# Sums over partitions of an adaptive-norm modulation: TensorE columns, or accumulating transfers in DRAM on GpSimd's queue

## What is computed

```python
c_act = jax.nn.silu(c)
mod = (c_act @ mod_w[layer] + mod_b[layer]).reshape(B, N_SUB, 3, D_MODEL)   # first block, 3 sublayers a layer
shift, scale, gate = mod_j[:, 0], mod_j[:, 1], mod_j[:, 2]
h = rmsnorm(x, g) * (1 + scale[:, None, :]) + shift[:, None, :]             # a sublayer's input
x = x + MACARON_W * g * swiglu(h, ...)                                      # g = 1 + gate
mod = c_act @ ada_w[i] + ada_b[i]                                           # second block, 2 sublayers a layer
```

## Time and profile before

| | |
|---|---|
| median of 3 runs | 2444.95 us |
| the profiled execution | 2440.32 us |
| its span, first to last instruction | 2438.7 us |
| TensorE busy, granted clock | 93% of the span, 0.947 |
| VectorE, ScalarE, GpSimd busy | 67%, 50%, 15% |
| DMA engines, mean | 219 GB/s, 65% of 16 engines' time |
| TensorE's share of the chain that ended last | 83% |

### The profile page before, as it was taken

The page is one execution under the profiler, slowest core; times in us unless marked ns, Lnnn a source line. Parts: engine busy times, 40 slices in busy tenths (PEclk is TensorE's granted clock), DMA queues, the critical chain, the costliest instruction groups (busy, mean ns, idle before and its releaser), DMA issues.

```text
span 2438.7 us, 37573 instructions
## 1 busy us (share of the span) xinstructions
PE 2262.4 (93%) x14486; PEld 2054.7 (84%) x14486; DVE 1635.7 (67%) x1943; ACT 1216.4 (50%) x1898; POOL 366.2 (15%) x513
## 2 busy tenths in 40 slices
PE   2999999999999995999988999998999799998998
PEld 2998977998999894898866998987987798876987
DVE  6677754767776755766875776775766776654654
ACT  2544455544553454544554554535545554565543
POOL 0111100111121003111000120800210221000210
PEclk9999999999999997999977999999999899988999
DMA  8789872878897951798664578512778378441653
GB/s 326 258 287 325 284 256 91 283 266 319 262 320 257 281 189 43 253 316 284 213 240 143 176 265 277 180 35 87 242 288 247 98 255 287 133 131 54 188 198 104
DMA packets 295522, 532.98 MB, mean 219 GB/s; under 512 B 10065, under 2 KB 185564, under 8 KB 295388
## 3 DMA queue, kind: packets, MB, share of 16 engines
q1 hardware_dynamic: 262396, 358.05, 44.8%
q0 software_dynamic: 32992, 173.09, 20.0%
HBM read 530.00 MB, written 1.11 MB: 218 GB/s over the span
## 4 chain that ended last, share of the span: by engine, by line
PE 83%; DVE 7%; ACT 5%; issue 3%; DMA 2%; SPq 0%; POOL 0%; DVEq 0%; ACTq 0%
PE bk L1340 12%; PE bk L1341 12%; PE bk L1342 12%; PE bk L1239 9%; PE bk L1241 9%; PE bk L1240 8%; PE bk L1391 4%; PE bk L1589 2%; PE bk L1284 1%; DVE w_lo L1706 1%; PE bk L1227 1%; PE bk L1229 1%; PE bk L1228 1%; DVE mod_acc L1725 1%; PE bk L1317 1%
## 5 line engine op out<-in xcount | busy, mean ns | idle before, releaser
L1706 DVE TENSOR_TENSOR w_lo<-raw,w_hi 128x1024 fp32r<-128x1024 f32 (+5 forms) x720 | 833.2, 1186 | 520.9 <-ACT w_hi L791 519.3
L791 ACT ACTIVATE w_hi<-raw 128x1024 fp32r<-128x1024 f32 (+5 forms) x720 | 683.0, 976 | 683.0 <-PE bk L1241 335.7
L1340 PE MATMUL bk<-a_hi,w_hi 128*128 128x256 f32 x2332 | 665.0, 285 | 5.2 <-DVE a_lo L1791 5.2
L1341 PE MATMUL bk<-a_lo,w_hi 128*128 128x256 f32 x2332 | 663.5, 285 | 0.0
L1342 PE MATMUL bk<-a_hi,w_lo 128*128 128x256 f32 x2332 | 663.2, 284 | 0.0
L1340 PEld LDWEIGHTS bk<-a_hi,w_hi 128*128 128x128 f32 x2332 | 451.6, 194 | 6.5 <-DVE a_lo L1791 4.0
L1341 PEld LDWEIGHTS bk<-a_lo,w_hi 128*128 128x128 f32 x2332 | 451.6, 194 | 0.0
L1342 PEld LDWEIGHTS bk<-a_hi,w_lo 128*128 128x128 f32 x2332 | 451.4, 194 | 0.0
L1725 DVE SCALAR_TENSOR_TENSOR mod_acc<-mod_raw,cact,mod_acc 128x1536 f32<-128x1536 f32 x182 | 329.9, 1813 | 35.4 <-DMA mod_raw<-in_ada_w 20.4
L1241 PE MATMUL bk<-w_hi,hid_lo 128*128 128x512 f32 x832 | 327.4, 394 | 0.0
L1239 PE MATMUL bk<-w_hi,hid_hi 128*128 128x512 f32 x832 | 324.3, 390 | 3.0 <-DVE w_lo L1706 3.0
(11 more groups left out here) (341 smaller groups left out, 3221.9 us busy)
## 6 DMA issues: line engine op xcount, KB each, us to landing
raw<-in_ffn_w SPq DMA_DIRECT2D x128, 1024.0 KB, 5.8
mod_raw<-in_ada_w POOLq DMA_DIRECT2D x128, 768.0 KB, 6.2
raw<-in_ffn_w_gu SPq DMA_DIRECT2D x88, 1024.0 KB, 7.6
mod_raw<-in_mod_w POOLq DMA_DIRECT2D x80, 768.0 KB, 6.9
raw<-in_ffn_w_down SPq DMA_DIRECT2D x40, 1024.0 KB, 7.1
first_mod<-in_mod_w SPq DMA_DIRECT2D x16, 768.0 KB, 10.0
raw<-in_sb_w_qkv SPq DMA_DIRECT2D x12, 1024.0 KB, 6.6
raw<-in_conv_w_pw SPq DMA_DIRECT2D x12, 1024.0 KB, 5.5
```

The source lines that it names most:

```text
L791: ins = act.activation(o(w_hi[:, p % OPS, :]), r(raw[:, c % RAWS, :]), ACT.Copy)
L1340: pe.matmul(o, wh, a_hi[:, f, :], start=(f == 0), stop=False)
L1341: pe.matmul(o, wh, a_lo[:, f, :], start=False, stop=False)
L1706: ins = dve.tensor_tensor(o(w_lo[:, p % OPS, :]), r(raw[:, c % RAWS, :]), o(w_hi[:, p % OPS, :].bitcast(F32)), ALU.subtract)
```

## The change

Groups 1 to 13 no longer go through the 24 products. When a group's 16 units are in, GpSimd stores mod_acc (1.5 MB) to a DRAM buffer folds, 128 rows of 3072. Seven transfers within DRAM then add the lower half of the remaining rows to the upper half, with an accumulating DMA on GpSimd's queue: 64 rows onto 64, then 32, 16, 8, 4, 2 and 1. A ninth transfer loads the single row that is left as a tile mod_row of 24 rows x 128, and TensorE transposes that tile into 24 PSUM columns. Each of the nine steps waits on the queue for the one before it. Group 0 keeps the 24 products.

```diff
+        mod_row = sb("mod_row", [MODC // P, P])
+        folds = nc.dram_tensor("folds", (2, P, MODC), F32).ap()
+        fold_done = sem("fold_done")
+        STEPS = 9
...
+            def fold(g, i):
+                if g is None:
+                    return
+                if i == 0:
+                    pool.wait_ge(mod_used, 2 + UNITS * (g + 1))
+                    if g > 1:
+                        pool.wait_ge(fold_done, 16 * STEPS * (g - 1))
+                    pool.dma_start(folds[g % 2], mod_acc[:, :]).then_inc(fold_done, 16)
+                    return
+                pool.wait_ge(fold_done, 16 * (STEPS * (g - 1) + i))
+                if i == STEPS - 1:
+                    pool.wait_ge(mod_ready, g)
+                    pool.dma_start(mod_row[:, :], folds[g % 2, 0].rearrange("(j p) -> j p", p=P)).then_inc(fold_done, 16)
+                    return
+                n = P >> i
+                wide = min(MODW, n * MODC // 16)
+                flat = folds[g % 2].rearrange("k f -> (k f)")
+                upper, lower = (flat[a * MODC:(a + n) * MODC].rearrange("(q f) -> q f", f=wide) for a in (0, n))
+                pool.dma_start(upper, lower, accum_op=ALU.add, max_dma_last_dim=4 * MODW).then_inc(fold_done, 16)
...
+            def mod_sum(g, w):
+                is_free(pe, w)
+                if g == 0:
...
+                else:
+                    pe.wait_ge(fold_done, 16 * STEPS * g)
+                    ins = pe.transpose(mod_out(w), mod_row[:, :], ident[0:MODC // P, 0:MODC // P])
+                ins.then_inc(turn_done, 1)
+                k.add("turn", 1)
```

The ffn1 stage on GpSimd's queue, and VectorE's new wait before it overwrites mod_acc:

```diff
-                    mod_rest(g, lambda i, b: hid_low(n + 2 * i + b, 2 * i + b, b))
+                    for j in range(KD):
+                        mod_next(g, j + 1)
+                        hid_low(n + j, j, j % 2)
+                        fold(st["late"], j + 1)
+                    fold(g, 0)
                     for b in range(3):
                         if b:
                             mod_next(g + 1, b)
                         hid_low(n + 8 + b, 8 + b, b % 2)
+                        fold(g, b + 1)
                     gate_tile(st["n"])
...
-                    for r in range(3, KD):
+                    for i in (4, 5, 6):
+                        fold(g, i)
+                    mod_next(g + 1, 3)
+                    for i in (7, 8):
+                        fold(g, i)
+                    for r in range(4, KD + 1):
                         mod_next(g + 1, r)
-                    mod_next(g + 1, KD)
+                    fold(g + 1, 0)
...
                 if isinstance(r, int) and r == 0:
+                    if g >= 2:
+                        dve.wait_ge(fold_done, 16 * (STEPS * (g - 2) + 1))
                     dve.tensor_scalar(a, src, cc[:, 0:1], None, ALU.mult).then_inc(mod_used, 1)
```

On TensorE the call moves from the start of a stage, and from job 8 of ffn1, into later jobs; keep_busy takes its place at the start:

```diff
-                if st["late"]:
-                    mod_sum(st["late"], w)
-                elif g:
+                if g:
+                    turned()
                     is_free(pe, w)
-                    keep_busy(job_banks(w)[:, 3, :], 16 if after(g) == "post" else 6)
+                    keep_busy(job_banks(w)[:, 3, :], 16 if after(g) == "post" else 8)
...
+                    if beside is not None and q == n // 2:
+                        mod_sum(beside, w - 1)
...
-                        gate_up(c + 2 * b, w + b, 0, second=(lambda: mod_sum(st["groups"][0], w + 9)) if b == 8 else None)
+                        gate_up(c + 2 * b, w + b, 0, second=(lambda: mod_sum(st["late"], w + 10)) if b == 9 and st["late"] else None)
...
-                    job(c + 28, w + 12, 0, H, 0, 22, None, by_token(w + 12), tail=True)
+                    job(c + 28, w + 12, 0, H, 0, 22, None, by_token(w + 12), tail=True, beside=st["groups"][0])
```

More of the change, by code:

```diff
@@ L376, in build @@
             late = stages[-1]["groups"][-1] if n and stages[-1]["groups"] else None
+            if "pool" in kinds[n - 1:n + 1] and n:
+                late = stages[9]["groups"][-1] if kind != "pool" else None
             stages.append(dict(kind=kind, n=n, c=c, w=w, hid=hid, groups=groups, late=late, nth=kinds[:n].count(kind)))
@@ L688, in two_low @@
                             hid_low(n + 4 * i + 2 * b + e, 4 * i + 2 * b + e, e)
-                    with pool.Fori(0, 4) as i:
+                    for i in range(4):
                         for b in range(2):
@@ L720, in _ @@
                         ins.then_inc(diag_ready, 1)
+                    for i in range(1, STEPS):
+                        fold(st["late"], i)
                     pool.wait_ge(ln_ready, 1)
@@ L760, in _ @@
                             gate_tile(st["n"])
+                    fold(st["groups"][0], 0)
                 elif st["kind"] == "lru":
                     pool.memset(lxb[:, :, 0:TAPS - 1], 0.0).then_inc(xb_zero, 1)
+                    for i in range(1, STEPS):
+                        fold(st["late"], i)
                     for n in range(NB):
@@ L1662, in _ @@
                     job(c + 12, w + 6, 0, A, 0, KD, None, by_token(w + 6))
-                    job(c + 14, w + 7, 0, A, 0, KD, None, by_token(w + 7), tail=True)
+                    job(c + 14, w + 7, 0, A, 0, KD, None, by_token(w + 7), tail=True, beside=st["late"])
                 elif st["kind"] == "lru":
@@ L1679, in _ @@
                     job(c + 10, w + 5, 0, A, 0, NB, lambda f: (lact_ready, f + 1), by_token(w + 5))
[L1680 removed]
+                    job(c + 13, w + 6, 0, A, 0, NB, None, by_token(w + 6), tail=True, beside=st["late"])
         @block.vector
@@ L1776, in a_values @@
                 tokens_normed(g)
-                if stages[g]["late"]:
-                    mod_finish(stages[g]["late"], w)
                 dve.wait_ge(mod_ready, g + 1)
@@ L1835, in second_half @@
             def second_half(g, w, c):
+                if stages[g]["late"] and kinds[g] != "ffn1":
+                    mod_finish(stages[g]["late"], w - 1)
                 for i in (2, 3):
@@ L2159, in _ @@
                                 mod_add(st["groups"][1], 4, 0)
+                        if m:
+                            mod_finish(st["groups"][0], w + 11)
                         if m:
```

53 lines of the change are left out of this document (21 added, 32 removed).

## The result

The changed kernel takes **2485.58 us** (median of 4 runs, 2484.27 to 2486.72) against 2445.49 for the kernel before (4 runs on the same chip): ratio 1.0172, 95% interval 1.0146 to 1.0198. It is 40 us slower where 15 us faster was forecast, and outside the range.

What follows compares the result with a forecast made beforehand. TensorE, 83% of the chain, was taken as the bound. Gain 45 less store 10, first accumulation 4 and hops 16 is 15 us off 2440.3, 2425; that execution stands 4.6 below the median, so 2430 us, range 2402 to 2464.

Steps and rivals of the forecast that it cites:

- What bounds it: TensorE holds 83% of the chain; the one-column products summing over partitions are TensorE time on the path.
- Job 8, 34 us: In job 8 of the four ffn1 stages, removing the sums and the slow clock behind them can give 34 us.
- Starts, 11.6 + 1.7: Removing the sums gains 11.6 us at starts of stages 1 to 4, 1.7 at starts behind a second norm.
- The store, 10 us: In ffn1 VectorE waits for the first group's store before the second group's mod_acc: 2.5 us a stage, 10 us.
- the late groups' stores: They add 1.5 MB at stage ends; taken at 0, at most 1 us each.
- The hops, 16 us: Behind ffn1's job 10, completions of steps 3, 4, 5 delay row block 3's load: 4 us a stage, 16 us.
- the first accumulation, 4: The 768 KB accumulation stands ahead of the next mod_raw load on the queue: 1 us a stage, 4 us.
- The cover: Behind ffn1's job 10, full slots of mod_raw pieces were to absorb 6.3 us of the load's 9.6 us delay.
- rival C: Chained completions ahead of ffn1's mod_raw load make it slower, 2467 at 53 us; sign: load over 15 us behind hid_low; chance 0.26.
- Elsewhere, 0: Outside ffn1's down projection, lru included, the steps have time and four weight buffers cover shared engines: 0 us.
- The clock: Sign in ffn1: TensorE's granted clock stays 1.00 through job 8.
- The estimate of 5 us a completion: Counter-rule for hops in ffn1: 5 us each with issue, 8.7 a stage, making the kernel some 4 us slower.

Runs made afterwards that it cites:

- e3b_nofolds: Changed kernel with store, accumulations and load of the 24 rows all left out, and no wait for a store: 2409.22 us, 0.9870 of the kernel before.
- e13_turn: e3_nosteps with the late group's turn in the middle of job 10 instead of job 9: 2425.53 us, 0.9929 of the kernel before.
- e14_small: e3_nosteps with a store of 16 of the 128 partitions, every wait kept: 2416.44 us, 0.9892 of the kernel before.
- e7_twohops: Changed kernel with two chained 12 KB copies added ahead of accumulation 4 in each ffn1 stage: 2511.46 us, 1.0278 of the kernel before.
- e8_acc1: e3_nosteps with accumulation 1 alone (768 KB) put back: 2441.95 us, 0.9994 of the kernel before.
- e1_order: Changed kernel with row block 3's load ahead of accumulation 4 in ffn1, accumulations 4 to 8 each behind a load: 2458.72 us, 1.0065 of the kernel before.
- e3_nosteps: Changed kernel with each group's seven accumulations left out, store, row load, turn and waits kept: 2430.69 us, 0.9959 of the kernel before.
- e16_split: e6_fewer with the middle group's accumulation 1 behind row block 1's loads, a wider identity tile and the store in two halves: 2432.27 us, 0.9955 of the kernel before.
- e17_end: e16_split with the two new tiles placed behind all others in on-chip memory: 2421.30 us, 0.9911 of the kernel before.
- e2_store: Changed kernel with ffn1's store ahead of GpSimd's subtraction for block 7 and late accumulations one place earlier: 2486.55 us, 1.0183 of the kernel before.
- e6_fewer: e5_lru with four accumulations instead of seven, the 8 rows left summed and turned by two matmuls: 2453.70 us, 1.0031 of the kernel before.
- e5_lru: e1_order with the late turn in job 10 and lru's accumulations held until the first two jobs' weights are used: 2461.93 us, 1.0079 of the kernel before.

## Why the prediction was wrong, point by point

- **What bounds it: right.** The sums were TensorE time on the path, and taking them away for nothing is worth 32 us (e3b_nofolds).
- **Job 8, 34 us: too high.** From the product of job 7 to that of job 10, e3b_nofolds has 34.4, 39.0, 39.0 and 34.6 us in stages 0, 2, 3 and 5 where the three ideal jobs are 34.56; against before's 40.6, 44.0, 44.6 and 43.0 that is 25 us, not 34. The missing 9 are stages 2 and 3, where I let the late group's transpose into job 9 at 0.16 us and mod_finish behind it at half a microsecond. In e3b_nofolds, where no store delays VectorE, TensorE stands still 2.50 us for mod_finish in each of the two, and right behind that the granted clock is 0.69 of full, part of that time at 1.2 instead of 2.4 GHz (us, busy PE, PEld, DVE, ACT, POOL, PEclk, DMA share, GB/s):

```profile
528.00:532.00 4.00, 2.08 (x14) 2.08 (x15) 3.42 (x6) 1.00 (x2) 0.00 (x0) 0.89 0.87 278
532.00:536.00 4.00, 4.00 (x26) 4.00 (x26) 0.84 (x2) 1.69 (x2) 1.80 (x2) 0.69 0.80 244
```

  In stage 0, which has no such turn, the clock stays 1.00 there. So a turn in job 9 costs 4.4 us with everything else for nothing. "I am wrong if TensorE waits at the transposes" was in the text; it was a term and should have been priced.
- **Starts, 11.6 + 1.7: about right.** By the reading of the earlier trace rows stages 3 and 5 now start alike, 24.2 us both, as forecast. The other 10 us of e3b_nofolds' 35 in ffn1 lie in its first jobs and in the sums that start the stages behind, in the cut used here; the ten stages of other kinds add up to within 1 us of before.
- **The store, 10 us: 22.** Its wait was seen (8.3 us in stage 2, 7.3 in 3, 1.9 and 2.9 in 0 and 5), and its place on the queue too. Two things were not: in stages 2 and 3 the wait goes on to TensorE through the turn (e13_turn, 5 and 6 us), and the late groups' stores, taken at 0 to 1 us, cost 6 us at the start of lru alone (147.8 against 141.6 in e14_small), where they meet its weights.
- **The hops, 16 us, and the first accumulation, 4: together 52.** This is the step that failed: "3.2 a hop, and the load comes 9.6 us later", then "9.6 - 6.3 = 3.3 us". The price of a small completion was right, 3.2 us by e7_twohops. But the accumulations of 192 to 48 KB under load took 3.44, 5.59 and 3.75 us to land on the chain, where I had 2.7. So in stage 2 the load goes out 15.4 us behind hid_low ("more than 15 is C") and not 1.8 as before: 13.6 us later, not 9.6. The cover was smaller than 6.3: VectorE's wait of 12.60, 12.21, 12.68 and 14.35 us in stages 0, 2, 3 and 5 becomes one of 9.41, 6.58, 7.06 and 11.08 on TensorE, so 3.2 to 5.6 us were absorbed. Where I took 4 us a stage, 6.6 to 11.1 were lost at this place. Order alone is 26 us, which is rival C's mechanism at half of its 53. Accumulation 1's bytes are 9 (e8_acc1) where I took 4. The last 17 of the 52 are the other accumulations' traffic and what hangs on it; no run takes them apart by cause. By place, of the 25 us between the profiles of e1_order and e3_nosteps, accumulation 1's among them, 4 are in lru and 21 in ffn1, about half of those behind the product of job 10.
- **Elsewhere, 0: wrong in lru**, by 8.7 us: a store, then an accumulation of 768 KB, and 1.3 MB of small weights share the engines with its first large weights, and SyncE's four buffers did not cover it. The chain of the changed kernel there has one piece that says so:

```profile
864.64 20.06 DMA raw<-in_lru_w_in
```

- **The clock** was not 1.00 through job 8. It read 0.88 from 531 to 541 us, with TensorE busy 4.01 of the 10 us in its wait for the store; the earlier trace rows had 0.67 and 0.65 with the sums.

The estimate of 5 us a completion made the forecast some 4 us slower than before, the right sign. The Trainium skill, "DMA: Bandwidth & Descriptors", section Latency and other measured facts, has a memory access grow from 0.2 to 2 us at high load; the pieces on the chain, 3.4 to 5.6 us, agree with some growth, the added copies at 3.2 show little of it, and neither accounts for most of the 40 us.

## What to carry to other kernels

A chain of transfers that wait for each other costs its latency in everything that stands behind it on the queue: put each step behind a load that has to wait anyway, and ask whether fewer steps with a little more arithmetic will do. When compute is taken away from a stretch whose DMA engines are already 0.9 busy, megabytes are no longer free, and a store that an engine waits for should stand behind no step that waits itself, and go out in the pieces in which its data become final. A new wait is priced by following it from the engine that waits to the instruction of the bounding engine that needs it, two steps on, not by its own length.

## What the runs showed of the hardware

- The place of tiles in on-chip memory changes TensorE's speed. With hid_hi and hid_lo 128 bytes higher in each partition than before, all three products of the ffn2 down projection take 395 to 396 ns; in their old place and 1024 bytes lower, 388, 392 and 394. The other tile that they read, w_hi or w_lo, does not move between the two kernels. That is 1.7 us in stage 13 and 6.8 us over the four ffn2 stages (e16_split against e17_end). What in the address does it is open: 96, 128, 0 and -1024 bytes are the shifts of the declared tiles in these kernels, and -512 in the changed kernel, whose stage 13 has 191.99.
- In the stages without a late group a 1.5 MB store issued 2 us earlier landed no earlier (10.6 and 12.4 us behind its issue for 8.7 and 9.9, e2_store). Issued some 6 us earlier, in stage 2 of e6_fewer against e5_lru, it landed 2.6 us earlier; in two halves, as they became final, in time in all four ffn1 stages.
- Within DRAM, adding takes longer than copying: 768 KB land in 8.1 us (median of 13) when added and in 5.3 when copied.
- A stretch can be full at a low rate: 0.81 of the engines busy at 138 GB/s with an accumulation and a load in flight, 0.89 at 295 GB/s without the accumulation.
